# Weight slots of a split fp32 matmul stream, moved within SBUF by 64 and 128 bytes

## The chip, the cores and the metric

The kernel runs on one core of one Trainium2 chip. The metric is the device time of one execution in microseconds (us), and the median of several runs is compared.

## What is computed

The reference is one inference step of a four-layer trunk for two groups of tokens at once: 256 tokens of a prompt and 32 tokens of a sample, 1024 features wide. Layers 0 and 3 mix tokens by an mLSTM, layer 1 by stick-breaking attention, layer 2 by multi-head latent attention. Each layer ends with an MLP of 4096 hidden features. Cut to what matters here:

```python
for i in range(4):
    h = rmsnorm(x, norm_mix[i])
    x = x + mixer[i % 3](h)          # projections h @ w, then attention or recurrence, then @ w_down
    h = rmsnorm(x, norm_mlp[i])
    x = x + square(relu(h @ w_ff1[i])) @ w_ff2[i]     # 1024 -> 4096 -> 1024
```

Everything is float32. Most of the work is the products with the weights, each used once for all 288 tokens.

## The kernel before

All activations stay in SBUF, features on the partitions and the T = 288 tokens side by side, so a block of 128 features is 288 float32 in each partition: `BLK` = 1152 bytes. To keep float32 accuracy at the speed of TensorE's rounded type fp32r, every operand is split in two fp32r parts, a high one and a low one: `XGH` and `XGL` for the inputs of a layer's first product (8 blocks each), `HH` and `HL` for hidden values (32 blocks each), `WHI` and `WLO` for weights. A product is the sum of three: high by high, low by high, high by low.

The stream of weights has four steps. SyncE loads tiles of 256 x 512 weights into four places of `RAWT`. ScalarE rounds one block of 128 x 512 into a slot of `WHI` (L651). VectorE subtracts that from the raw weights into the slot of `WLO` (L1056). There are `SPL` = 4 slots of each, and one block in one slot is called a unit. TensorE then runs `unit` (the matmul is issued at L1773 by the helper `mm`):

```python
for a, (c, m) in enumerate(cols):          # four times 128 weight columns, 512 bytes apart
    mm(out, WHI[:, slot, c:c + m], rh, start, False)
    mm(out, WHI[:, slot, c:c + m], rl, False, False)
    ins = mm(out, WLO[:, slot, c:c + m], rh, False, stop)
```

Here `rh` and `rl` are the high and the low part of one block of activations, `XGH[:, k, :]` or `HH[:, k, :]`. They are the moving operand, 288 columns; the weights are the stationary operand. A unit is thus twelve matmuls of 128 x 288, each with a load of 128 x 128 weights before it. Each product runs over its blocks k in order, and unit and slot go round with k, so that slot = k mod 4 nearly everywhere (the query projection of layer 2 has three units in a group).

The order of all work is written out by hand in one program for each engine, with semaphores between. ScalarE waits for the unit that last used a slot, VectorE for ScalarE, TensorE for VectorE.

All addresses in SBUF are laid out by hand too: `take` hands out the next bytes, rounded up to 32. From the start of `XGH` to the start of `WHI` there are 2 x 8 blocks, 64 blocks and 16384 bytes of raw weights, together 108,544 bytes or 424 times 256; `HH` lies 90,112 bytes or 352 times 256 ahead of `WHI`. The low parts lie whole multiples of 256 behind the high ones. A slot is 2048 bytes, 8 times 256; a block of 1152 bytes is 4.5 times 256.

Of the kernel before, what the change touches and what calls it, by code (L numbers as in the profile page):

```python
# [5 lines left out]
F32R = mybir.dt.float32r  # L6
# [8 lines left out]
TP, TS = 256, 32  # L15
T = TP + TS
# [10 lines left out]
P = 128  # L27
# [6 lines left out]

RAW = 4
SPL = 4


class Stage:
# [69 lines left out]
def hybrid_trunk_kernel(nc, d, o):  # L109

    ctx = ExitStack()
    with ctx:
# [3 lines left out]
        def at(name, shape, offset, dt=F32):  # L116
            return nc.alloc_sbuf_tensor_at(name, shape, dt, offset=offset)

        def take(nbytes):
            off = place[0]  # L120
            place[0] += ((nbytes + 31) // 32) * 32
            return off

        BLK = 4 * T
        I4 = at("I4", [P, TS], take(4 * TS))
        o_x, o_xg, o_h = take(DB * BLK), take(2 * DB * BLK), take(64 * BLK)
        o_raw, o_hi, o_lo = take(RAW * 4096), take(SPL * 2048), take(SPL * 2048)
        o_mix, o_cp = take(32 * BLK + 24576), take(4096)
        o_tmp = take(4 * 294 * 4)
        X = at("X", [P, DB, T], o_x)  # L130
# [2 lines left out]
        HH = at("HH", [P, 32, T], o_h, F32R)  # L133
        HL = at("HL", [P, 32, T], o_h + 32 * BLK, F32R)
        RAWT = at("RAWT", [P, RAW, 1024], o_raw)
        WHI = at("WHI", [P, SPL, 512], o_hi, F32R)
        WLO = at("WLO", [P, SPL, 512], o_lo, F32R)
        TMPX = at("TMPX", [P, 4, 294], o_tmp)
        TMP = at("TMP", [P, 4, T], o_tmp)
        IDENT = at("IDENT", [P, P], take(512))  # L140
        ONES = at("ONES", [P, P], take(512))
        COLS = at("COLS", [P, NCOL], take(NCOL * 4))
        RSTD = at("RSTD", [P, T], take(BLK))
        R = at("R", [4, 2 * T + TS], take(4 * (2 * T + TS)))
        AECOL = at("AECOL", [P, 29], take(4 * 29))
        D4 = at("D4", [4, 4], take(16))
        HB4 = at("HB4", [P, 4], take(16))
# [195 lines left out]
        def nope_in(ap):  # L343
            return ap.rearrange("p (h e) -> p h e", h=4)[:, :, 0:CNOPE]

        def nope_out(ap):
            return ap[:, 0:4 * CNOPE].rearrange("p (h e) -> p h e", h=4)
# [280 lines left out]
        def _(act):  # L628
# [7 lines left out]
            def split(st, j, c):  # L636

                if st.upt == 2:
# [5 lines left out]
                    u = st.u0 + 8 * j + c  # L644
                    if not isinstance(u, int) or u >= SPL:
                        act.wait_ge(unit_done, 8 * j + (st.u0 + c - SPL + 1))
                    w = WIDTH.get(st.name, 512)
                    hi, raw = WHI[:, c % SPL, 0:w], RAWT[:, slot, kk * w:(kk + 1) * w]
                    if st.name == "ukv":
                        hi, raw = by_part(hi), by_head(raw)  # L650
                    act.activation(hi, raw, ACT.Copy).then_inc(weight_hi, 1)  # L651
                else:
                    n, s = st.n0 + c, (st.u0 + c) % SPL
                    act.wait_ge(weight_in[n % RAW], 16 * (n // RAW + 1))
                    act.wait_ge(unit_done, st.u0 + c - SPL + 1)
                    hi, raw = WHI[:, s, 0:4 * CQD], RAWT[:, n % RAW, 0:4 * CQD]
                    act.activation(nope_out(hi), nope_in(raw), ACT.Copy)
# [375 lines left out]
        def _(dve):  # L1033
            own = [0]

            def link(ins):
                own[0] += 1
                ins.then_inc(dve_own, 1)
                dve.wait_ge(dve_own, own[0])

            def over4(ap, n=4):

                return ap.unsqueeze(1).to_broadcast([P, n, ap.shape[-1]])

            def split(st, j, c):

                if st.upt == 2:
# [3 lines left out]
                    dve.wait_ge(weight_hi, 8 * j + (st.u0 + c + 1))  # L1051
                    lo, hi = WLO[:, c % SPL, 0:w], WHI[:, c % SPL, 0:w].bitcast(F32)
                    raw = RAWT[:, c // 2, (c % 2) * w:(c % 2 + 1) * w]
# [3 lines left out]
                else:  # L1057
                    n, s = st.n0 + c, (st.u0 + c) % SPL
                    dve.wait_ge(weight_hi, st.u0 + c + 1)
                    lo, hi = WLO[:, s, 0:4 * CQD], WHI[:, s, 0:4 * CQD].bitcast(F32)  # L1060
                    raw = RAWT[:, n % RAW, 0:4 * CQD]
# [17 lines left out]
            def newton(out, v, y, t):  # L1079

                link(dve.scalar_tensor_tensor(t, y, 1.0, y, ALU.mult, ALU.mult))
                link(dve.scalar_tensor_tensor(t, t, -0.5, v, ALU.mult, ALU.mult))
                link(dve.scalar_tensor_tensor(out, t, 1.5, y, ALU.add, ALU.mult))
# [10 lines left out]
            def scale(nu):  # L1094
                dve.wait_ge(y_out, nu + 1)
                newton(RSTD[:], NV[:], NY[:], NT[:])

# [55 lines left out]
            def mlstm_up(i, la):  # L1153
                st = ST["up", i]

                def after(g, b):
# [11 lines left out]
                    if g % 2 == 0:  # L1168
                        if x:
# [5 lines left out]
                                        COLS[:, c0:c0 + 48].rearrange("p (j b) -> p b j", j=3)[:, 4 * x:4 * x + 4, :])  # L1175
                        dve.tensor_tensor(TMPX[:, :, 3:259], bank[:, :, 0:TP], over4(RSTD[:, 0:TP]), ALU.mult)
                        link(dve.tensor_tensor(TMPX[:, :, 262:294], bank[:, :, TP:T], over4(RSTD[:, TP:T]), ALU.mult))
                        for s, c in ((0, 256), (1, 291)):
# [3 lines left out]
                    else:  # L1182
                        dve.tensor_tensor(SIGZ[:, 4 * x:4 * x + 4, :], bank[:, :, 0:T], over4(RSTD[:]),
                                          ALU.mult).then_inc(group_out, 1)
# [39 lines left out]
            def mlstm_mix(i, la, evac_last):  # L1224
# [18 lines left out]
                                            ALU.max, ALU.max))  # L1243
                link(dve.scalar_tensor_tensor(R[:, T:2 * T], E, -1.0, B, ALU.mult, ALU.subtract))
                link(dve.scalar_tensor_tensor(R[:, 2 * T:2 * T + TS], E[:, TP:T], -1.0,
                                              SMALL[:, 4 + la:5 + la].to_broadcast([4, TS]), ALU.mult, ALU.add))
                dve.tensor_scalar(D4[:], IDENT[0:4, 0:4], R[:, 2 * T + TS - 1:2 * T + TS], None,
                                  ALU.mult).then_inc(rows_out, 1)
                dve.tensor_scalar(R[:, 0:T], E, -1.0, None, ALU.mult).then_inc(rows_out, 1)
                if la:  # L1250
                    dve.wait_ge(m_dma, 32 * la)
                dve.tensor_scalar(SMALL[:, 6:7], R[:, T + TP - 1:T + TP], -1.0, None, ALU.mult)
                dve.tensor_scalar(SMALL[:, 7:8], R[:, 2 * T - 1:2 * T], -1.0, None, ALU.mult).then_inc(m_out, 1)
                dve.wait_ge(acol_done, la + 1)
# [184 lines left out]
            def sb_qkv(i):  # L1439
                st = ST["bqkv", i]  # L1440

                def after(x, b):
# [5 lines left out]
                    if m == 0:  # L1448
                        ins = dve.scalar_tensor_tensor(BQ[:, 4 * half:4 * half + 4, :], bank, float(BDH) ** -0.5,
                                                       over4(RSTD[:]), ALU.mult, ALU.mult)  # L1450
                    else:
                        dst = (BK if m == 1 else BV)[:, 4 * half:4 * half + 4, 0:T]
                        ins = dve.tensor_tensor(dst, bank, over4(RSTD[:]), ALU.mult)
                    ins.then_inc(group_out, 1)
# [316 lines left out]
        def _(pe):  # L1771
            def mm(out, lhsT, rhs, start=True, stop=True, **kw):
                return pe.matmul(out, lhsT, rhs, start=start, stop=stop, **kw)  # L1773
# [9 lines left out]
            def unit(u, slot, b, cols, rh, rl, start, stop, var=None):  # L1783

                pe.wait_ge(weight_lo, u + 1)
                for a, (c, m) in enumerate(cols):
                    if a == 2 and var is not None:
                        pe.wait_ge(var_out, var + 1)
                    out = PS[0:m, 4 * b + a, 0:rh.shape[-1]]
# [3 lines that stand above are left out]
                ins.then_inc(unit_done, 1)  # L1793
# [452 lines left out]
            def mla_up(i):  # L2246
# [44 lines left out]
                for t in range(4):  # L2291
# [4 lines left out]
                    for a in range(2):  # L2296
                        c, out = slice(P * a, P * (a + 1)), PS[:, a, 0:TK]
                        for k in range(2):
                            mm(out, WHI[:, S[k], c], CKH[:, k, :], k == 0, False)
                            mm(out, WHI[:, S[k], c], CKL[:, k, :], False, False)  # L2300
                            ins = mm(out, WLO[:, S[k], c], CKH[:, k, :], False, k == 1)
                    ins.then_inc(ukv_done, 1)
# [8 lines left out]
                    for kb, s0, n in ((0, 0, P), (1, P, P), (2, T, P), (3, TP, TS)):  # L2311
                        out = PS[0:n, 4 + kb, 0:256]
                        for k in range(2):
                            wh, wl = (w[:, S[k], 256:512] for w in (WHI, WLO))
                            mm(out, CKH[:, k, s0:s0 + n], wh, k == 0, False)
# [217 lines left out]
```

## Time and profile before

| | |
|---|---|
| median of 3 runs | 1811.24 us (1809.86 to 1812.17) |
| time of the profiled execution | 1812.56 us |
| its span, first to last instruction | 1810.5 us |
| TensorE busy | 98% of the span |
| VectorE, ScalarE, GpSimd busy | 63%, 48%, 9% |
| mean granted TensorE clock | 0.995 of full speed |

The profile comes from one execution; the times from runs like it. A matmul's own duration in the profile is the time from its start to its modelled end. Matmuls overlap, so the pace of the stream is read from the distance between their starts, not from the durations.

### The profile page before, as it was taken

The page shows a single profiled execution, that of the slowest core. Times are in us where ns is not written, and L with a number is a line of the kernel's source. Part 1 is how long each engine was busy: PE and PEld are TensorE (multiplying, and loading weights), DVE is VectorE, ACT ScalarE, POOL GpSimd, SP SyncE. Part 2 cuts the span into 40 slices and gives each one's busy share as a digit, 9 for nine tenths or more (in the row PEclk, how much of TensorE's full clock was granted, in tenths as well). Part 3 has the DMA queues.
Part 4 walks back from the last instruction along what each step waited for, and adds up shares of the span by engine and source line. Part 5 has one row for each costly group of instructions (what it writes and reads, how often), then busy time and mean ns, then how long its engine had stood idle before and what let it go on. Part 6 is the DMA issues. An engine that isn't in the chain of part 4 may idle for free.

```text
span 1810.5 us, 33987 instructions
## 1 busy us (share of the span) xinstructions
PE 1770.1 (98%) x13177; PEld 1648.0 (91%) x13177; DVE 1141.2 (63%) x1856; ACT 875.8 (48%) x1470; POOL 160.2 (9%) x111
## 2 busy tenths in 40 slices
PE   7999999999999999999999999999999999999997
PEld 6999855999999979999997799999999964999997
DVE  4886577575556546664566675555887568666543
ACT  4565422455444385554454555544565422455443
POOL 0000132110011002000120020011000034110000
PEclk9999999999999999999999999999999999999998
DMA  4566334655555514555543155555455424555552
GB/s 150 166 164 175 100 116 163 190 163 165 169 164 170 188 60 154 163 163 166 168 117 113 49 162 165 170 164 163 151 161 174 142 85 161 187 163 162 167 169 86
DMA packets 155883, 272.94 MB, mean 151 GB/s; under 512 B 22693, under 2 KB 28274, under 8 KB 155770
## 3 DMA queue, kind: packets, MB, share of 16 engines
q1 hardware_dynamic: 155770, 271.37, 47.8%
q8 instruction: 79, 1.29, 0.3%
q14 instruction: 34, 0.28, 0.1%
HBM read 250.55 MB, written 20.78 MB: 150 GB/s over the span
## 4 chain that ended last, share of the span: by engine, by line
PE 88%; DVE 7%; ACT 3%; issue 1%; DMA 1%; SPq 0%; ACTq 0%; DVEq 0%
PE PS L1773 86%; PE PS L1778 2%; ACT PB L949 1%; DVE C L1325 1%; DVE WLO L1056 1%; DVE QT L1360 0%; DVE NB L1316 0%; DMA XIN<-in_x_sample_dram 0%; DVE TMP L1635 0%; DMA RAWT<-in_c_w_ukv_dram 0%; DVE QT L1365 0%; DVE BST L1302 0%; DVE KS L1292 0%; DVE HL L1371 0%; ACT QCP L814 0%
## 5 line engine op out<-in xcount | busy, mean ns | idle before, releaser
L1056 DVE TENSOR_TENSOR WLO<-RAWT,WHI 128x512 fp32r<-128x512 f32 (+1 forms) x904 | 636.6, 722 | 490.6 <-ACT WHI L651 488.6
L651 ACT ACTIVATE WHI<-RAWT 128x512 fp32r<-128x512 f32 (+1 forms) x904 | 554.7, 626 | 653.7 <-PE PS L1773 651.3
L1773 PE MATMUL PS<-XGH,WHI 128*128 128x288 f32 x1776 | 527.2, 297 | 6.2 <-DVE WLO L1056 6.1
L1773 PE MATMUL PS<-HH,WLO 128*128 128x288 f32 (+1 forms) x1792 | 528.7, 295 | 0.0
L1773 PE MATMUL PS<-HH,WHI 128*128 128x288 f32 (+1 forms) x1792 | 527.9, 295 | 0.4 <-issue 0.4
L1773 PE MATMUL PS<-HL,WHI 128*128 128x288 f32 (+1 forms) x1792 | 527.6, 294 | 0.0
L1773 PE MATMUL PS<-XGH,WLO 128*128 128x288 f32 x1776 | 525.6, 296 | 0.0
L1773 PE MATMUL PS<-XGL,WHI 128*128 128x288 f32 x1776 | 524.5, 295 | 0.0
L1773 PEld LDWEIGHTS PS<-XGH,WHI 128*128 128x128 f32 x1776 | 334.3, 188 | 9.9 <-DVE WLO L1056 6.8
L1773 PEld LDWEIGHTS PS<-HH,WHI 128*128 128x128 f32 x1792 | 336.1, 188 | 3.7 <-issue 3.6
L1773 PEld LDWEIGHTS PS<-HH,WLO 128*128 128x128 f32 x1792 | 336.1, 188 | 0.0
L1773 PEld LDWEIGHTS PS<-HL,WHI 128*128 128x128 f32 x1792 | 336.1, 188 | 0.0
L1773 PEld LDWEIGHTS PS<-XGL,WHI 128*128 128x128 f32 x1776 | 334.1, 188 | 0.2
L1773 PEld LDWEIGHTS PS<-XGH,WLO 128*128 128x128 f32 x1776 | 334.1, 188 | 0.2
L1697 POOL TENSOR_TENSOR SQ<-X 128x1152 f32<-128x1152 f32 x13 | 32.7, 2515 | 892.9 <-DVE X L1068 547.3
L1773 PE MATMUL PS<-VTOK,KG 128*128 128x512 f32 x128 | 60.8, 605 | 0.8 <-ACT QCP L814 0.8
L999 ACT ACTIVATE TMP<-TMP 128x1152 f32<-128x1152 f32 x32 | 37.4, 1168 | 23.2 <-DVE TMP L1635 23.2
L1635 DVE SCALAR_TENSOR_TENSOR TMP<-PS,RSTD 128x1152 f32<-128x1152 f32 x32 | 43.4, 1358 | 6.8 <-PE PS L1773 6.7
L1773 PEld LDWEIGHTS PS<-VTOK,KG 128*128 128x128 f32 x128 | 22.2, 190 | 26.1 <-issue 24.9
L1644 DVE TENSOR_TENSOR HL<-TMP,HH 128x1152 f32 (+1 forms) x32 | 43.3, 1353 | 2.9 <-ACT HH L1001 2.9
L1141 DVE SCALAR_TENSOR_TENSOR CV__90<-TMPX,COLS,CV__90 128x291 f32<-128x291 f32 x96 | 43.6, 518 | 0.0
L665 ACT ACTIVATE XGH<-X,COLS 128x288 fp32r<-128x288 f32 x64 | 29.1, 525 | 23.6 <-DVE X L1113 12.9
(364 smaller groups left out, 1415.6 us busy)
## 6 DMA issues: line engine op xcount, KB each, us to landing
RAWT<-in_w_ff_dram SPq DMA_DIRECT2D x256, 512.0 KB, 3.7
RAWT<-in_a_w_up_dram SPq DMA_DIRECT2D x64, 512.0 KB, 3.7
RAWT<-in_a_w_down_dram SPq DMA_DIRECT2D x32, 512.0 KB, 3.7
RAWT<-in_b_w_qkv_dram SPq DMA_DIRECT2D x24, 512.0 KB, 3.8
RAWT<-in_a_w_q_dram SPq DMA_DIRECT2D x16, 512.0 KB, 3.7
RAWT<-in_a_w_k_dram SPq DMA_DIRECT2D x16, 512.0 KB, 3.6
RAWT<-in_a_w_v_dram SPq DMA_DIRECT2D x16, 512.0 KB, 3.7
C<-in_state_mlstm_C_dram SPq DMA_DIRECT2D x8, 1024.0 KB, 5.8
```

The costliest lines, as they stand in the source:

```text
L651: act.activation(hi, raw, ACT.Copy).then_inc(weight_hi, 1)
L665: ins = act.activation(XGH[:, f, :], X[:, f, :], ACT.Copy, scale=COLS[:, gain(nu) + f:gain(nu) + f + 1])
L949: ins = act.activation(PB[:, p % 3, a, k0:k0 + n], PS[:, b0 + a, k0:k0 + n], ACT.Exp, bias=c[:, 1, a, x:x + 1], scale=CVQ[:, 4, x:x + 1], ...
L999: act.activation(TMP[:], TMP[:], ACT.Square).then_inc(h_sq, 1)
L1056: dve.tensor_tensor(lo, raw, hi, ALU.subtract).then_inc(weight_lo, 1)
L1141: ins = dve.scalar_tensor_tensor(CV_[:, a, 0:291], TMPX[:, a, j:j + 291], COLS[:, w0:w0 + 1], CV_[:, a, 0:291], ALU.mult, ALU.add)
L1325: ins = dve.scalar_tensor_tensor(C0[:, h % 2, b, :], C0[:, h % 2, b, :], AECOL[:, 25 + h:26 + h], PS[:, bank, :], ALU.mult, ALU.add)
L1635: dve.scalar_tensor_tensor(TMP[:], PS[:, 4 * b:4 * b + 4, 0:T], 0.0, over4(RSTD[:]), ALU.max, ALU.mult).then_inc(group_out, 1)
L1644: dve.tensor_tensor(HL[:, bass.ds(4 * g, 4), :], TMP[:], HH[:, bass.ds(4 * g, 4), :].bitcast(F32), ALU.subtract).then_inc(h_lo, 1)
L1697: link(pool.tensor_tensor(SQ[:], x, x, ALU.mult))
L1773: return pe.matmul(out, lhsT, rhs, start=start, stop=stop, **kw)
L1778: return pe.transpose(out, in_, IDENT[0:n, 0:n])
```

## The change

The slots of `WHI` and `WLO` are laid 2176 bytes apart instead of 2048, and both tensors begin 64 bytes later than a multiple of 256 from the activations. A slot still holds 512 float32; the 128 bytes behind them are not used. The two tensors grow by 1088 bytes together. To make room, `R`, a small work tile of the mLSTM gates on 4 partitions, is laid over `RSTD`, the reciprocal norms.

```diff
+SLOT = 2048 + 128
...
-        o_raw, o_hi, o_lo = take(RAW * 4096), take(SPL * 2048), take(SPL * 2048)
+        o_raw, o_hi, o_lo = take(RAW * 4096), take(64 + SPL * SLOT) + 64, take(SPL * SLOT)
...
-        WHI = at("WHI", [P, SPL, 512], o_hi, F32R)
-        WLO = at("WLO", [P, SPL, 512], o_lo, F32R)
+        WHI = at("WHI", [P, SPL, SLOT // 4], o_hi, F32R)
+        WLO = at("WLO", [P, SPL, SLOT // 4], o_lo, F32R)
...
-        RSTD = at("RSTD", [P, T], take(BLK))
-        R = at("R", [4, 2 * T + TS], take(4 * (2 * T + TS)))
+        o_rstd = take(4 * (2 * T + TS))
+        RSTD = at("RSTD", [P, T], o_rstd)
+        R = at("R", [4, 2 * T + TS], o_rstd)
```

No engine gets another instruction, another order, another shape or another wait: row by row the five programs name the same operations on the same tiles. What differs is where tiles lie. `WHI` and `WLO` move as said. Each tile allocated behind them moves by 1088 bytes, 64 more than a multiple of 256: the mixers' work area (`SIGZ`, `KT`, `VTOK`, `QN`, `KN`, ...), `TMP`, `IDENT`, `ONES`, `COLS`, `RSTD`; `AECOL` and the small tiles behind it move back by 64. `X`, `XGH`, `XGL`, `HH`, `HL`, `RAWT` and all that is laid over them stay.

The distance from a moving block to its weight slot, modulo 256 bytes, is this:

| block k | moving block starts at | slot before | distance before | slot after | distance after |
|---|---|---|---|---|---|
| even | 0 | 0 | 0 | 64 | 64 |
| odd | 128 | 0 | 128 | 192 | 64 |

## Rows read from the trace of the kernel before

**Rows 1.** The page: busy time of each engine, and the granted clock in 40 slices.
```profile
PE 1770.1 (98%) x13177; PEld 1648.0 (91%) x13177; DVE 1141.2 (63%) x1856; ACT 875.8 (48%) x1470; POOL 160.2 (9%) x111
...
PEclk9999999999999999999999999999999999999998
```

**Rows 2.** The page: the chain of work that ended last, by engine and line.
```profile
PE 88%; DVE 7%; ACT 3%; issue 1%; DMA 1%; SPq 0%; ACTq 0%; DVEq 0%
PE PS L1773 86%; PE PS L1778 2%; ACT PB L949 1%; DVE C L1325 1%; DVE WLO L1056 1%; DVE QT L1360 0%; DVE NB L1316 0%; DMA XIN<-in_x_sample_dram 0%; DVE TMP L1635 0%; DMA RAWT<-in_c_w_ukv_dram 0%; DVE QT L1365 0%; DVE BST L1302 0%; DVE KS L1292 0%; DVE HL L1371 0%; ACT QCP L814 0%
```

**Rows 3.** The page's costliest groups: operation, count, busy, mean ns, idle before.
```profile
L1056 DVE TENSOR_TENSOR WLO<-RAWT,WHI 128x512 fp32r<-128x512 f32 (+1 forms) x904 | 636.6, 722 | 490.6 <-ACT WHI L651 488.6
L651 ACT ACTIVATE WHI<-RAWT 128x512 fp32r<-128x512 f32 (+1 forms) x904 | 554.7, 626 | 653.7 <-PE PS L1773 651.3
L1773 PE MATMUL PS<-XGH,WHI 128*128 128x288 f32 x1776 | 527.2, 297 | 6.2 <-DVE WLO L1056 6.1
L1773 PE MATMUL PS<-HH,WLO 128*128 128x288 f32 (+1 forms) x1792 | 528.7, 295 | 0.0
```

**Rows 4.** Timeline of TensorE near the start: start, duration, operation.
```profile
17.02 0.44 PE L1773 MATMUL PS<-XGH,WLO 128*128 128x288 f32 x1
17.26 0.44 PE L1773 MATMUL PS<-XGH,WHI 128*128 128x288 f32 x1
17.50 0.44 PE L1773 MATMUL PS<-XGL,WHI 128*128 128x288 f32 x1
...
23.06 0.29 PE L1773 MATMUL PS<-XGH,WLO 128*128 128x288 f32 x1
23.19 0.29 PE L1773 MATMUL PS<-XGH,WHI 128*128 128x288 f32 x1
23.32 0.30 PE L1773 MATMUL PS<-XGL,WHI 128*128 128x288 f32 x1
```

**Rows 5.** The chain in order of time: its two longest pieces without a break.
```profile
376.37 199.59 PE PS L1773 x1504
...
1609.38 173.59 PE PS L1773 x1308
```

**Rows 6.** Timeline, last layer's second MLP product: first matmul of blocks 0 to 4.
```profile
1693.77 0.29 PE L1773 MATMUL PS<-HH,WHI 128*128 128x288 f32 x1
1693.89 0.29 PE L1773 MATMUL PS<-HL,WHI 128*128 128x288 f32 x1
1694.03 0.30 PE L1773 MATMUL PS<-HH,WLO 128*128 128x288 f32 x1
...
1695.34 0.30 PE L1773 MATMUL PS<-HH,WHI 128*128 128x288 f32 x1
...
1696.95 0.29 PE L1773 MATMUL PS<-HH,WHI 128*128 128x288 f32 x1
...
1698.53 0.29 PE L1773 MATMUL PS<-HH,WHI 128*128 128x288 f32 x1
...
1700.13 0.29 PE L1773 MATMUL PS<-HH,WHI 128*128 128x288 f32 x1
```

**Rows 7.** The same product forty units later: five first matmuls of units, twelve rows apart.
```profile
1757.37 0.29 PE L1773 MATMUL PS<-HH,WHI 128*128 x1
...
1758.94 0.30 PE L1773 MATMUL PS<-HH,WHI 128*128 x1
...
1760.55 0.29 PE L1773 MATMUL PS<-HH,WHI 128*128 x1
...
1762.13 0.29 PE L1773 MATMUL PS<-HH,WHI 128*128 x1
...
1763.73 0.29 PE L1773 MATMUL PS<-HH,WHI 128*128 x1
```

**Rows 8.** Timeline in layer 2: 24 matmuls of 256 columns, stationary blocks from CKH and CKL.
```profile
968.31 0.28 PE L1773 MATMUL PS<-WHI,CKH 128*128 128x256 f32 x1
...
970.45 0.28 PE L1773 MATMUL PS<-WHI,CKH 128*32 128x256 f32 x1
...
971.15 0.38 PE L1778 MATMUL PS<-IDENT,CKV 128*128 128x128 f32 x2
```

**Rows 9.** Whom TensorE waited for: us in total, times, longest us.
```profile
PE PS L1773 <- DVE WLO L1056: 6.1, 11, 1.6
PE PS L1778 <- DMA XIN<-in_x_sample_dram: 4.5, 1, 4.5
PE PS L1773 <- issue: 3.5, 4, 2.6
```

## The prediction, made before the changed kernel was timed

> **What bounds the kernel now.** I read the page's busy times first. TensorE is busy for 98% of the span, and its clock stands at its upper level in all slices but the last, where it dips a little [rows 1]. Then I read the chain of waits: 88% of it is TensorE, and 86% are matmuls of the one line through which all products go [rows 2]. The table of waits shows no engine that holds TensorE up: the weights cost it 6.1 us in 11 waits [rows 9]. ScalarE needs 626 ns for a block of weights and VectorE 722 ns, and both stand idle for about 500 to 650 us in all between blocks, waiting for slots or for each other [rows 3]. So the time is the number of matmuls by their pace, and only a change of that pace can matter.
>
> How many: the rounded product has 3 x 1776 matmuls with XGH or XGL and 3 x 1792 with HH or HL, of which [rows 3] shows one kind each. That is 10,704 matmuls, or 892 units of twelve.
>
> What pace: with the clock at its lower level, 1.2 GHz, at the start of the program, starts are 0.24 us apart, exactly one cycle for each of 288 columns, as its first three rows show [rows 4]. With the clock at 2.4 GHz the same matmuls would be 0.12 us apart if columns alone set the pace. The last three rows show them 0.13 us apart [rows 4]; over 1504 in a row 199.59 / 1504 = 132.7 ns, over 1308 in a row 173.59 / 1308 = 132.7 ns [rows 5]. Some 12.5 ns in each matmul are not columns, and they appear only at the high clock. Over 10,704 matmuls that is 134 us. This is what a change of addresses could touch, since at the high clock TensorE asks SBUF for its operands twice as fast.
>
> By the Trainium skill ("TensorE: Matmul & The Clock Gate", Back-to-back issue gap) a matmul of N columns follows the last after N / 2.4 + 2.5 ns, which is 122.5 ns here. The trace has 132.7 ns, so it disagrees, and the measurement decides.
>
> **The change, part by part.** It adds and removes no instruction on any engine, so there is nothing to count there. It has three parts.
>
> *1. The distance from moving block to weight slot.* Now it is 0 for even blocks and 128 bytes for odd ones; afterwards it is 64 for all. The trace shows whether that distance has gone along with the pace at all, because it changes from unit to unit. In the last layer's second MLP product the first matmul of block 0 starts at 1693.77, of block 1 at 1695.34, of block 2 at 1696.95, of block 3 at 1698.53, of block 4 at 1700.13 [rows 6]. Even blocks took 1.57 and 1.58, odd ones 1.61 and 1.60. Forty units later it is 1.57, 1.61, 1.58, 1.60 again [rows 7], and the 40 units between took 63.60, or 1.59 each. So this is a fixed pattern and no noise. The mean of the four even units is 6.30 / 4 = 1.575 us, of the four odd ones 6.42 / 4 = 1.605 us. The difference is 0.030 us for a unit, known to about 0.01, since the rows are rounded to 0.01.
>
> No row shows a distance of 64, so its price has to be bounded. From below the cost: a unit can't be quicker than twelve times the column time, 12 x 0.12 = 1.44 us, which gives 892 x (1.59 - 1.44) = 134 us of gain. From above: the longest single step in the unit shown is 0.14 us, from the second row to the third [rows 6], and twelve of those are 1.68 us, a loss of 892 x 0.09 = 80 us. These ends are far apart. The nearest rows are the two kinds of unit themselves. If 64 behaves as 0 does, the odd units win 0.030 and the even ones nothing: 446 x 0.030 = 13.4 us. If it behaves as 128 does, the even units lose that: 13.4 us the other way. I take the quicker kind. The reason is a choice and not a proof: within a unit whose distance is fixed, steps of 0.12 and 0.14 follow each other [rows 6], so the extra time is made of collisions that come and go. A distance of 128 is the furthest from the quick kind that there is, and 64 is half-way; and each unit at one and the same distance also spares the stream the change of pattern at every unit border.
>
> *2. The tiles behind the slots.* They all move by 64 modulo 256, and so TensorE's f32 work in the mixers reads other places: KT, VTOK, IDENT, ONES. The time outside the 892 units is 1810.5 - 892 x 1.59 = 392 us. No row gives a pace of such an operation at two places. The kinds of unit above differ by 2% at most; 1% of 392 us would be 4 us either way. I take nothing, and keep 4 us for the range. ScalarE's 626 ns and VectorE's 722 ns for a block [rows 3] would have to grow together past the 1590 ns of a unit before TensorE saw it; their sum now is 1348 ns. If that cover were gone, each nanosecond beyond would count 892 times.
>
> *3. R over RSTD.* R is written while the mLSTM gates are worked out, after the up-projection has used RSTD and before the MLP's norm is written; no wait is added. It costs nothing. RSTD itself is read by 32 operations at the ends of groups, not in the stream.
>
> The sum against the profiled execution is 1812.56 - 13.4 = 1799.2 us. That execution is 1.3 us above the median of the runs, so the forecast for the median is 1811.24 - 13.4 = **1798 us**.
>
> **The rivals.** *No change.* The place of the weights may not matter at all, and the odd units may be slower because their moving block starts at 128, which stays so. For it speaks a row with other proportions: 18 matmuls of 256 columns with stationary blocks of 128 columns took 970.45 - 968.31 = 2.14 us, 119 ns each, and 6 with stationary blocks of only 32 columns took 971.15 - 970.45 = 0.70 us, 117 ns each [rows 8]. Columns alone would be 256 / 2.4 = 107 ns. With a quarter of the weights to load, 10 of 12 extra nanoseconds stay. If most of the extra time doesn't come from the loads, where they read may not matter either. Against it: within one unit the moving block is always the same while steps of 0.12, 0.13 and 0.14 follow in a fixed order, so something besides the moving block takes part. Time: 1811, and within 3.6 us of it, which is 0.2% and about what a measurement of this kernel tells from no change. Chance 0.26.
>
> The Trainium skill says this more strongly ("TensorE: Matmul & The Clock Gate", Step-by-step: what each phase is for): TensorE has two independent read ports into SBUF, one for the moving operand and one for the weights, so that loading the next weights doesn't steal bandwidth from the running matmul. By that rule the change does nothing, and the sum stays 1812.56 us for the profiled execution. No row before settles whether it holds at 4 bytes in each cycle of 2.4 GHz.
>
> *A large gain.* If 64 bytes keep the two streams off each other all along, a third or more of the extra 0.15 us of a unit could go: 892 x 0.05 = 45 us, which gives 1767 us, and at the very end 1677. For it speaks that an extra 12.5 ns exist only at the high clock; against it the 32-column row, where little of it hangs on the loads. Chance 0.12, half of it beyond 1772.
>
> *Slower.* 64 bytes may be on the wrong side: every unit goes at the pace of the odd ones, 446 x 0.030 = 13.4 us more, 1825 us. This decides as soon as a unit at distance 64 takes over 1.594 us, which is 3.6 us over 892 units more than now. Nothing in the trace excludes it: two distances were seen, and what lies between two points of a cycle is not known to lie between their times. With a further step beyond the odd ones it would be 1838. Chance 0.22, a third of it beyond 1826.
>
> **How the numbers follow.** The forecast has 0.40: units at the pace of the even ones or a little better, with an own range of 1784 to 1806 (from 0.04 us saved in each odd and 0.01 in each even unit, with 4 us for the moved tiles, to 0.01 us in each odd unit). Faster by over 0.2%: that and the large gain, less a small part that falls within, 0.51. Within 0.2%: 0.27. Slower: 0.22. The range that leaves out the ends of the two outer cases is 1772 to 1826.
>
> **What would show it.** In the trace after, starts of units read as above: even and odd blocks take the same time, 1.57 to 1.58 us, and the long pieces of the chain go at about 131.3 ns a matmul instead of 132.7. The count of instructions, the waits for weights of some 6 us and ScalarE's and VectorE's mean durations stay. If odd units are still 0.03 us behind even ones, the weight's place is not what set their pace, and the rule of the two ports has won. If all units take 1.60 or more, the direction was wrong. If a unit takes 1.54 or less, the extra time was collisions after all, and I priced them too low.

## The result, and the profile after

The change made the kernel a little slower: 1816.29 us against 1812.44 us for the kernel before, medians of 14 runs each, ratio 1.0021 with a 95% interval of 1.0013 to 1.0029. The medians understate the difference, because the time of one and the same kernel goes along with the mean granted clock of its run. In the runs of the kernel before that were taken beside the last four experiments it is 1819.0 us in the one with 0.990 and 1810.6 us (median of 9) in those with 0.997. The changed kernel's eight runs with 0.997 have a median of 1816.3 us, 5.7 more, though the two sets were not taken side by side. The profiled execution took 1816.58 us, with a span of 1814.5 us.

First the page of the kernel after: busy times, and two of the costliest groups (the lines of the code are two further down than before).

```profile
PE 1772.9 (98%) x13177; PEld 1650.7 (91%) x13177; DVE 1142.1 (63%) x1856; ACT 876.2 (48%) x1470; POOL 160.6 (9%) x111
...
L1058 DVE TENSOR_TENSOR WLO<-RAWT,WHI 128x512 fp32r<-128x512 f32 (+1 forms) x904 | 636.3, 721 | 496.7 <-ACT WHI L653 494.1
L653 ACT ACTIVATE WHI<-RAWT 128x512 fp32r<-128x512 f32 (+1 forms) x904 | 555.4, 626 | 659.0 <-PE PS L1775 656.1
```

The instruction counts are those of [rows 1], and VectorE and ScalarE take 721 and 626 ns for a block, within 1 ns of [rows 3]; they only stand idle 5 to 6 us longer. TensorE's waits, from the table of waits of the kernel after:

```profile
PE PS L1775 <- DVE WLO L1058: 6.0, 11, 1.6
PE PS L1780 <- DMA XIN<-in_x_sample_dram: 4.9, 1, 4.9
PE PS L1775 <- issue: 3.5, 4, 2.6
```

They are those of [rows 9], but for 0.4 us more in the wait for the first input. So nothing waits longer in the stream; the matmuls themselves come at another pace. The chain in order of time shows it, in the same two pieces as [rows 5]:

```profile
377.58 200.39 PE PS L1775 x1504
...
1613.41 174.31 PE PS L1775 x1308
```

200.39 us instead of 199.59, and 174.31 instead of 173.59: 0.53 and 0.55 ns more for a matmul. Some other long pieces grew a little less. Both traces list the same matmuls in the same order, and from start to start the 10,704 of the stream take some 5.5 us more in the one after. The ratio of the times, 0.21%, is at the edge of what was called a difference.

The span grew by 4.0 only. The first input came 0.4 us later, and the profiled execution of before had two short stretches at the lower clock in the last layer that the one after had not. The rows are busy times of a window, the column behind POOL is the granted clock; first the kernel before, then the one after, at the first of the two stretches:

```profile
1451.00:1455.50 4.50, 4.50 (x22) 4.12 (x23) 1.75 (x6) 1.74 (x4) 4.06 (x3) 0.62 0.00 0
```

```profile
1451.00:1460.00 9.00, 8.51 (x83) 6.88 (x82) 6.38 (x20) 3.73 (x8) 3.83 (x3) 1.00 0.01 3
```

In the first stretch sixteen transposes start 0.213 us apart before and 0.109 us after. What that gave back is read from the lag of the same matmul in the one trace behind the other: 4.73 us at the first of these transposes (1451.78 before, 1456.51 after) and 3.79 us once they and the matmuls next to them are done. The saving of 1.6 us is not kept whole, since in the kernel after TensorE then waits 0.49 us for VectorE. The second stretch, at 1800.3 us, where the granted clock of before is 0.50, brings the lag from 4.80 (1800.29 and 1805.10) to 3.92 us. So 5.5 + 0.4 - 0.9 - 0.9 is about 4.1, where the spans differ by 4.0. Last, the timeline after at the place of [rows 6], the first matmul of blocks 0 to 4:

```profile
1698.14 0.29 PE L1775 MATMUL PS<-HH,WHI 128*128 128x288 f32 x1
...
1699.74 0.29 PE L1775 MATMUL PS<-HH,WHI 128*128 128x288 f32 x1
...
1701.34 0.29 PE L1775 MATMUL PS<-HH,WHI 128*128 128x288 f32 x1
...
1702.93 0.29 PE L1775 MATMUL PS<-HH,WHI 128*128 128x288 f32 x1
...
1704.53 0.29 PE L1775 MATMUL PS<-HH,WHI 128*128 128x288 f32 x1
```

Even and odd blocks now take the same, 1.60, 1.60, 1.59, 1.60, and four units 6.39 us. Before they took 1.57, 1.61, 1.58, 1.60 and together 6.36. The difference between odd and even is gone, but the even ones went up by 0.02 and the odd ones came down by less than 0.01.

### The profile page after: what moved, and what is told of

Same layout as the page of the kernel before. It is cut to its first block, busy times and chain, and to the rows that moved or that the text cites. A ratio compares the mean times of both kernels' runs of the same rounds, so it can differ in the third digit from the quotient of the medians.

```text
span 1814.5 us, 33987 instructions
## 1 busy us (share of the span) xinstructions
PE 1772.9 (98%) x13177; PEld 1650.7 (91%) x13177; DVE 1142.1 (63%) x1856; ACT 876.2 (48%) x1470; POOL 160.6 (9%) x111
## 4 chain that ended last, share of the span: by engine, by line
PE 88%; DVE 7%; ACT 3%; issue 1%; DMA 1%; SPq 0%; ACTq 0%; DVEq 0%
PE PS L1775 86%; PE PS L1780 2%; ACT PB L951 1%; DVE C L1327 1%; DVE WLO L1058 1%; DVE QT L1362 0%; DVE NB L1318 0%; DMA XIN<-in_x_sample_dram 0%; DMA RAWT<-in_c_w_ukv_dram 0%; DVE TMP L1637 0%; DVE QT L1367 0%; DVE BST L1304 0%; DVE KS L1294 0%; DVE HL L1373 0%; ACT QCP L816 0%
```

## The experiments

All kernels start from the changed one and differ in the line of offsets (and in `SLOT`, where said). Distance means the address of a unit's weight slot minus that of its moving block, modulo 256 bytes. In the table "1504" and "1308" are the two pieces of the chain quoted above, in us; they are the most exact measure of pace. Each ratio is the recorded one, to runs of the kernel before taken beside that experiment (medians 1811.28 us for e1 to e4, 1812.30 for e5 to e8, 1811.32 for e9 to e12), and so not the quotient of two numbers of the table. e5_dist224 and e6_dist160 have 4 runs, e7_dist32 has 5, e4_dist192 has 7 and the others 9 to 14. Means of a unit are read from the starts of matmuls in the steady part of a stretch, to the nanosecond: 1.577 us answers to 172.1 in the last column, 1.590 to 173.6, 1.597 to 174.3, 1.603 to 175.0.

| kernel | distance | time, us | ratio to before (95%) | 1504 | 1308 |
|---|---|---|---|---|---|
| before | 0, 128 in turn | 1812.44 | | 199.59 | 173.59 |
| the change | 64 | 1816.29 | 1.0021 (1.0013 to 1.0029) | 200.39 | 174.31 |
| e1_dist0 | 0 | 1807.25 | 0.9972 (0.9961 to 0.9984) | 199.54 | 173.55 |
| e7_dist32 | 32 | 1820.25 | 1.0047 (1.0032 to 1.0062) | 200.38 | 175.03 |
| e2_dist64_tiles_back | 64 | 1816.77 | 1.0018 (1.0005 to 1.0031) | 200.37 | 174.31 |
| e11_dist320 | 64 (320 of 512) | 1816.37 | 1.0025 (1.0012 to 1.0037) | 200.38 | 174.31 |
| e3_dist128 | 128 | 1816.12 | 1.0018 (1.0004 to 1.0031) | 200.39 | 174.29 |
| e6_dist160 | 160 | 1802.57 | 0.9949 (0.9929 to 0.9969) | 198.09 | 172.14 |
| e4_dist192 | 192 | 1804.95 | 0.9953 (0.9936 to 0.9971) | 199.20 | 172.15 |
| e5_dist224 | 224 | 1822.30 | 1.0058 (1.0036 to 1.0080) | 201.18 | 175.03 |
| e8_all_by_64 | 0, 128 in turn | 1812.24 | 0.9997 (0.9984 to 1.0010) | 199.59 | 173.59 |
| e12_shift64_only | 64, 192 in turn | 1812.53 | 1.0008 (0.9999 to 1.0018) | 199.97 | 173.93 |
| e9_high160_low64 | high 160, low 64 | 1811.23 | 1.0004 (0.9992 to 1.0015) | 199.61 | 173.58 |
| e10_high64_low160 | high 64, low 160 | 1814.14 | 1.0016 (1.0004 to 1.0028) | 200.38 | 172.85 |

### Distance 0 throughout

```diff
-        o_raw, o_hi, o_lo = take(RAW * 4096), take(64 + SPL * SLOT) + 64, take(SPL * SLOT)
+        o_raw, o_hi, o_lo = take(RAW * 4096), take(SPL * SLOT) + 0, take(SPL * SLOT) + 0
```

> Distance 0 in every unit, slots 2176 bytes apart, the tiles behind the slots at the phase they had before. If the distance from moving block to weight slot sets a unit's pace, odd units come down to the even units' 1.575 us, all units take about 1.578 us and the time is some 10 us below that of before, about 1802. If the odd units are slower because of where their moving block starts, they stay at 1.60 and the time stays at that of before, 1812. If a slot start other than a multiple of 256 costs something by itself, odd units get slower still.

Measured 1807.25 us, faster than before by 0.28%, but not 1802. Odd units did not come down to 1.578 in general. In the chain of this kernel two pieces of the same length and the same distances go at different paces:

```profile
375.80 199.54 PE PS L1775 x1504
...
1067.68 198.47 PE PS L1775 x1504
```

The first is as before the change (132.7 ns a matmul), the second is quicker (132.0), and in its steady part four units take 6.31 us. So the distance alone doesn't fix the pace; at one distance a stretch can fall into one of two regular patterns. Which one it is can even change inside a piece. In the quicker one a single step is long, from this start to the next at 1211.49, 0.22 us where 0.13 is usual:

```profile
1211.27 0.38 PE L1775 MATMUL PS<-HH,WHI 128*128 128x288 f32 x1
```

The four units before it take 6.30 us (starts at 1204.97 and 1211.27), and four units soon after it 6.36 us (1212.16 and 1218.52), at the same distance. e4_dist192 changes from 1.577 to 1.590 at the same place; e6_dist160 has such a step at 518.86 and stays at 1.577. What makes the long step was not found.

### The moved tiles

```diff
+        o_raw, o_hi, o_lo = take(RAW * 4096), take(SPL * SLOT) + 64, take(SPL * SLOT) + 64
```

The last 128 bytes of the last slot are unused, so the next tiles may begin there.

> The change with the tiles behind the slots put back to the phase that they had before; the distance of 64 stays. If the loss comes from the distance, the units take 1.5965 us as with the change and the time is 1816, 4 us above before. If the moved tiles cost the 4 us, it is 1812 and the time outside the units is shorter than with the change.

1816.77 us, and the same pieces of the chain as with the change. The loss comes with the distance. The tiles behind the slots, put back to their old phase, gave nothing that can be measured.

### Distance 128 and distance 192

```diff
+        o_raw, o_hi, o_lo = take(RAW * 4096), take(SPL * SLOT) + 128, take(SPL * SLOT) + 128
```

> Distance 128 in every unit. If the distance alone sets the pace, every unit takes what odd units took before, 1.60 us, or a little less in a steady run of equal units; the time is about 1812.5 + 446 x 0.023 = 1823. If the moving block's own start sets it, even units stay at 1.578 and the time at 1812.

1816.12 us, where 1823 was expected. Even units did get slower, so the moving block's own start, which is as before, is not what sets the pace. But a steady run at distance 128 takes 1.597 us a unit, exactly as at 64, and not the 1.60 or 1.61 that an odd unit took before between two even ones.

```diff
+        o_raw, o_hi, o_lo = take(RAW * 4096), take(SPL * SLOT) + 192, take(64 + SPL * SLOT) + 192
```

> Distance 192, that is the weights 64 bytes ahead instead of behind; the tiles behind the slots as in the change. If the pace depends on how far apart the two are on the circle of 256 bytes, the same on both sides, it is the 1.5965 us of distance 64 and the time is 1816. If the order of the two streams counts, it differs: below 1.578 us a unit it would be a better place than any seen (under 1802), above 1.60 a worse one.

1804.95 us, a ratio of 0.9953. The weights 64 bytes ahead are not the same as 64 behind. In the last product the first matmul of block 0 starts at 1689.25 and that of block 4 at 1695.56: 6.31 us for four units, against 6.36 in [rows 6] and 6.39 with the change. Other stretches of the same kernel go at 1.590 us a unit, among them most of the 1504 piece.

### Distances 224, 160 and 32

The same edit with 224, 160 and 32 (for 224 the tiles behind lie 96 bytes further than before modulo 256, for 160 64 bytes, for 32 not at all).

> Distance 224, the weights 32 bytes ahead. The runs so far show three paces only: 1577 us a thousand units (192, parts of 0), 1590 (before, parts of 0 and 192) and 1597 (64 and 128). If the quick side is the one where weights lie just ahead on the circle of 256 bytes, 224 lies between 192 and 0 and mixes 1577 and 1590, about 1804 us. If 192 is one lucky place, 224 goes at 1590 or 1597 throughout, 1811 to 1817.

> Distance 160, between 128 (1597) and 192 (1577 and 1590). With a smooth dependence on the distance all units take some 1590 and the time is about 1811. With paces that lock, it is one of the three known ones, and the border between slow and quick shows on which side of 160 it lies: 1817 if slow, 1805 if quick.

> Distance 32, between 0 (1577 and 1590) and 64 (1597). Slow, 1817 us, if every place where the weights lie behind the moving block on the circle is slow; 1807 if 32 is still as 0. A pace other than 1577, 1590 or 1597 would show that the locking to three values is false.

For 224 the expectation missed. 32 turned out slow, but slower than the 1817 of that case and at a new pace, which its last sentence had named as the sign that three values are not all. 160 turned out quick, as one of the cases had it, and a little quicker than its 1805. 224 is the slowest of all, 1822.30 us, although it lies between the two quick distances 192 and 0. 160 is the quickest, 1802.57 us, a ratio of 0.9949. 32 takes 1820.25 us, slower than both of its neighbours. And a fourth pace appeared, 1.603 us a unit. The timeline at the first matmul of blocks 0 and 4 of the last product, distance 224:

```profile
1702.66 0.30 PE L1775 MATMUL PS<-HH,WHI 128*128 128x288 f32 x1
...
1709.08 0.30 PE L1775 MATMUL PS<-HH,WHI 128*128 128x288 f32 x1
```

and distance 160:

```profile
1684.54 0.29 PE L1775 MATMUL PS<-HH,WHI 128*128 128x288 f32 x1
...
1690.85 0.29 PE L1775 MATMUL PS<-HH,WHI 128*128 128x288 f32 x1
```

6.42 us against 6.31. With 160 the chain is at the quick pace in all its long pieces:

```profile
375.27 198.09 PE PS L1775 x1504
...
1600.86 172.14 PE PS L1775 x1308
```

198.09 / 1504 = 131.7 ns and 172.14 / 1308 = 131.6 ns. No other distance tried did that. 96 is the one multiple of 32 that was not tried.

These kernels move the slots for every engine, so ScalarE's and VectorE's writes into them lie elsewhere too. The end of the last product parts the two: all weights are in their slots, and the other engines and the DMA queues stand still. The rows are busy times of a window, as above, for distance 160 and for 224:

```profile
1782.70:1787.20 4.50, 4.50 (x36) 4.50 (x36) 0.00 (x0) 0.00 (x0) 0.00 (x0) 1.00 0.00 0
```

```profile
1802.40:1807.00 4.60, 4.60 (x37) 4.60 (x36) 0.00 (x0) 0.00 (x0) 0.00 (x0) 1.00 0.00 0
```

The pace differs here as before: 27 matmuls take 3.55 us at 160 (starts at 1782.64 and 1786.19) and 3.61 us at 224 (1802.38 and 1805.99), 131.5 and 133.7 ns each. So the difference is there with TensorE working alone.

### Everything 64 bytes further

```diff
-SLOT = 2048 + 128
+SLOT = 2048
...
-        I4 = at("I4", [P, TS], take(4 * TS))
+        I4 = at("I4", [P, TS], take(64 + 4 * TS) + 64)
...
+        o_raw, o_hi, o_lo = take(RAW * 4096), take(SPL * SLOT) + 0, take(SPL * SLOT) + 0
```

> The slots of before (2048 apart, distances 0 and 128 in turn), with every tile in SBUF, activations and weights alike, 64 bytes further. If only the distance between the two counts, the unit pace is that of before, 1590 in the mean with 1.57 and 1.60 in turn, and the time 1811 to 1812. If the place of the weights itself counts, the pace changes, to 1597 if the loss of the change came from the weights starting at 64 and 192.

1812.24 us, ratio 0.9997, and both pieces of the chain are those of [rows 5] to the hundredth. For this shift absolute places don't matter, only where moving blocks and weights lie to each other. The pattern of [rows 6] comes two units later, though: to the nanosecond, blocks 0 to 3 of the same product take 1.581, 1.601, 1.576 and 1.602 us, where before they took 1.576, 1.602, 1.581 and 1.601. So the small difference between the two even units is not a matter of their addresses. The smaller `R` tile, which this kernel shares with the change, is also free.

### High and low weights apart

```diff
+        o_raw, o_hi, o_lo = take(RAW * 4096), take(SPL * SLOT) + 160, take(64 + SPL * SLOT) + 64
```

> High weights at distance 160, low weights at distance 64. Of twelve loads in a unit eight are of high weights. If each load costs by its own distance, the unit lies two thirds of the way from 1597 to 1577, at about 1584, and the time is about 1807. If the paces lock, it is 1577, 1590, 1597 or 1603 throughout. If only the low weights' place decides, it is 1597 and 1816.

and with 64 and 160 the other way round:

> The other way round: high weights at distance 64, low ones at 160. If each load costs by its own distance, about 1590 for a unit and 1811 us; if only the high weights count, 1597 and 1816; if only the low ones, 1577 and 1803.

High at 160 and low at 64 goes at 1.590 in both pieces, 1811.23 us. This is slower than the 1807 of loads that cost each by its own distance. High at 64 and low at 160 changes its pace between stretches, as its two pieces in the table show: 133.2 ns a matmul in the first and 132.1 in the second, which is a fifth pace, 1.583 us a unit. Neither the high nor the low weights alone decide. A sum of prices for each load gives neither result.

### 256 bytes further

```diff
+        o_raw, o_hi, o_lo = take(RAW * 4096), take(SPL * SLOT) + 320, take(192 + SPL * SLOT) + 320
...
-        BST = at("BST", [P, 2, 6], take(48))
-        MV = at("MV", [P, 2, 2], take(16))
+        BST = at("BST", [P, 2, 6], o_hi + 2048)
+        MV = at("MV", [P, 2, 2], o_hi + 2048 + 64)
```

> The weights 256 bytes further than in the change: distance 64 modulo 256, but 320 modulo 512. Two small tiles of layer norm statistics lie in the unused 128 bytes behind the first slot, to make room. If the rule is modulo 256, units take 1597 as with the change and the time is 1816. If the period is 512 or more, another pace appears; distance 0 and 128 of before were 0, 384, 256, 128 modulo 512 and took 1576, 1602, 1581 and 1601, which leaves a difference of 5 between 0 and 256 open.

1816.37 us, and 200.38 and 174.31 in the chain: the figures of the change. For this distance the pattern repeats with 256 bytes.

### The 64 bytes without the new stride

```diff
-SLOT = 2048 + 128
+SLOT = 2048
...
+        o_raw, o_hi, o_lo = take(RAW * 4096), take(SPL * SLOT) + 64, take(64 + SPL * SLOT) + 64
```

> Half of the change: the 64 bytes, but slots 2048 apart, so that even units are at distance 64 and odd ones at 192. If each unit has the price of its distance, it is 1597 and 1577 or 1590 in turn, in the mean about 1587 to 1593, and the time 1808 to 1813, better than the change. If the change of distance at every unit costs something by itself, the mean is above 1597.

1812.53 us, ratio 1.0008 (0.9999 to 1.0018), not told apart from before. Its 173.93 us lie half-way between the 173.59 of before and the 174.31 of the change, and the mean of a unit is 1.593 us: odd units, at distance 192, take 1.586, and even ones, at 64, take 1.600. So the new stride, which makes all distances equal, turned a mixture of 64 and 192 into the slow kind alone; at distance 0 the same stride gained.

## Why the prediction was wrong

**What bounds the kernel: right.** TensorE's pace and nothing else changed. Waits and the other engines' durations stayed, and the distance from moving block to weight slot acts on the pace. The rival by which the weights' place doesn't matter has fallen: from distance 224 to 160, with moving blocks untouched, the time goes from 1822.30 to 1802.57 us. One reading of the clock needs a correction. A digit 9 in [rows 1] hides short stretches at the lower clock: the granted clock is 0.50 from 36 to 38 us, from 1451.8 to 1455.2 and from 1800.3 to 1802.5. And where the first three rows of [rows 4] stand, the profile's granted clock reads 1.00; that they are at the lower clock follows from their spacing of 0.24 us alone, which is also the spacing at 36 us (36.11, 36.35, 36.59), where it reads 0.50. Neither touches the long pieces of the stream.

With that rival falls, for this stream, the sum by the Trainium skill's rule of two independent read ports ("TensorE: Matmul & The Clock Gate", Step-by-step: what each phase is for). That rule gives no difference; the runs show up to 20 us between places of the weights. The prediction's 122.5 ns, worked out from the Trainium skill ("TensorE: Matmul & The Clock Gate", Back-to-back issue gap), is what that section gives for a matmul by itself; for a stream with a weight load before each matmul it gives other figures, so the 132.7 ns here, with such a load before each, are no clean test of the formula. It entered no term.

**The step that failed** is part 1 of the working: "I take the quicker kind". The distance of 64 was given the price of distance 0. Measured, even units went from 1.575 to about 1.597 us, the odd ones from 1.605 to 1.597. The rows, rounded to 0.01, had made the difference between the kinds 0.030 us, where it is 0.023. With the trace's finer means of 1.5785 and 1.6015 us for even and odd units and 1.5965 for all after it, the sum is 446 x (+0.018 - 0.005) = +5.8 us, where -13.4 was forecast; the starts of the whole stream give 5.5. This was the slower rival at less than half of its price. Its threshold, a unit above 1.594 us, was passed by 0.003. Of the signs under "What would show it" none was met as written: even and odd units do take the same time, but 1.597 us, which is neither 1.57 to 1.58 nor "1.60 or more". The last of these comes nearest.

**The reasons given for that step** were wrong in two ways. One was that 64 is half-way between 0 and 128, and so a mild place. The pace isn't smooth in the distance: 0 is quick or middling, 32 slow, 64 and 128 alike, 160 and 192 quick, 224 slowest. The other was to read even units as the price of distance 0 and odd ones as the price of distance 128. Runs with one distance only give neither: at 0 most stretches stay at 1.590 us, at 128 it is 1.597, not 1.605. What [rows 6] and [rows 7] show is one pattern that repeats over four units, with a mean of 1.590; its parts have no price of their own. e9_high160_low64 says the same of the high and low loads.

**The moved tiles**: priced at nothing with 4 us kept; with them put back, e2_dist64_tiles_back takes 1816.77 us against 1816.29, so no cost was measured. **R over RSTD**: free, as e8_all_by_64 shows. **The range** held the measured time, which says little for the mechanism: it reached from a large gain to the slower rival, and the direction that came had a chance of 0.22.

**What stays open.** Why the distance acts as it does was not found. With one distance for all loads the stream has regular patterns with four different means (1.577, 1.590, 1.597, 1.603 us a unit); 1.583 came only in e10_high64_low160 and 1.593 only in e12_shift64_only, where distances are mixed. The distance decides which of them can occur. What puts a stretch into one of two possible patterns was not separated. That the pace can change at one long step, with all distances as they were, speaks for the time at which loads and matmuls meet, but no run varies that time on purpose. Nor was it tried why even the best kernel stays at 131.6 ns a matmul where 288 columns take 120. [Rows 8], with 32-column loads almost as slow as 128-column ones, speaks against a part that grows with the size of the loads, and the runs do not go beyond that.

The version that beats both is e6_dist160, the changed kernel with 160 bytes in the place of 64. It takes 1802.57 us (4 runs), a ratio of 0.9949 (0.9929 to 0.9969) to the kernel before.

## What to carry to other kernels

In this kernel, where matmuls follow each other without a wait and are slower than their columns at the high clock, the place of the two operands to each other in SBUF was worth half a per cent either way, and steps of 32 bytes in one offset found it. Whether it is worth as much with other shapes or types, no run here shows; a sweep is cheap. Do not interpolate between two distances, and do not take the parts of a repeating pattern for prices: make a stream with one distance only and read its pace from a long piece of the chain. To make all units alike is no gain by itself, since it makes them all slow at the wrong distance. And compare such small differences in pieces of the chain or in runs with the same granted clock: one short stretch at the lower clock hides a microsecond of them.

## What the runs showed of the hardware that was not expected

The pace of a stream of 128 x 288 matmuls with 128 x 128 loads, at the high clock, takes few values. With one distance the 1308 in a row came to 172.1, 173.6, 174.3 or 175.0 us, over seven distances modulo 256; with mixed distances 172.9 and 173.9 came too. The same addresses can give two of them in one execution, as 199.54 and 198.47 us for 1504 matmuls at distance 0 do, and the pace can change within a piece at one long step. The differences stay when no other engine and no DMA queue works: 131.5 ns a matmul at distance 160 and 133.7 at 224. Shifting both operands together by 64 bytes changes nothing, 199.59 and 173.59 us again; shifting the weights alone by 256 bytes reproduces the pace of distance 64.
